# Activations of 128 of 576 tokens from gathered rows of U, and an fp32 gate matrix stored on SP's queue

## The reference, cut to what matters

```
h = rms_norm(x + merged @ w_out)                       # 576 x 2048
s = scores of 8 heads x 2 halves against 128 keys      # top 16 of each, top 16 of the 256 pairs
experts[n, head, k]   (128 experts of 16384 a token), gate = softmax(top_s)
act  = gelu(h[n] . u[experts[n, head, k]])             # u: 16384 x 2048, fp32
out[n] = sum over head, k of gate * act * v[experts]   # v: 16384 x 2048, fp32
```

## Time and profile before

| | us |
|---|---|
| median of 3 runs | 4928.46 (4912.31 to 4931.71) |
| the profiled execution, its own time | 4921.65 |
| its span | 4919.6 |

### The profile page before, as it was taken

The page is one execution under the profiler, slowest core; times in us unless marked ns, Lnnn a source line. Parts: engine busy times, 40 slices in busy tenths (PEclk is TensorE's granted clock), DMA queues, the critical chain, the costliest instruction groups (busy, mean ns, idle before and its releaser), DMA issues.

```text
span 4919.6 us, 84579 instructions
## 1 busy us (share of the span) xinstructions
PE 4749.3 (97%) x35079; PEld 4510.0 (92%) x35079; DVE 2807.5 (57%) x5183; ACT 1217.3 (25%) x1483; POOL 780.0 (16%) x768
## 2 busy tenths in 40 slices
PE   8999999999999899999999999999999999999997
PEld 8999888888999899999999999999988888888887
DVE  3332643223343668878888863333366666776667
ACT  3212533322121212222222221212222222222223
POOL 1010012320000000000011000000054334434430
PEclk9999999999999999999999999999999999999999
DMA  6333246763445334434555554344488778877873
GB/s 191 104 112 99 64 158 216 235 202 102 134 128 144 71 72 105 109 100 118 131 141 141 133 133 109 102 106 107 162 318 304 303 302 302 310 265 302 305 298 110
DMA packets 474042, 842.18 MB, mean 171 GB/s; under 512 B 45201, under 2 KB 307345, under 8 KB 431512
## 3 DMA queue, kind: packets, MB, share of 16 engines
q1 hardware_dynamic: 400272, 502.55, 33.9%
q0 software_dynamic: 67968, 325.20, 19.0%
q10 hardware_dynamic: 5520, 10.49, 0.7%
HBM read 739.48 MB, written 94.14 MB: 169 GB/s over the span
## 4 chain that ended last, share of the span: by engine, by line
PE 80%; DMA 8%; DVE 6%; issue 3%; ACT 2%; SPq 1%; ACTq 0%; DVEq 0%
PE pair L1795 61%; PE pair L2218 10%; DMA v_raw<-in_peer_v_dram 7%; PE pair L1759 2%; DVE v_lo L1672 2%; PE pair L2199 2%; DVE main L1690 2%; ACT v_hi L1086 1%; PE pair L2152 1%; PE pair L1966 1%; ACT w_hi L776 1%; PE pair L1831 1%; PE pair L2009 1%; SPq L537 0%; PE pair L2106 0%
## 5 line engine op out<-in xcount | busy, mean ns | idle before, releaser
L1795 PE MATMUL pair<-act_hi,w_hi 128*128 128x288 f32 x7616 | 1653.9, 299 | 32.2 <-DVE act_lo L1219 12.1
L1795 PE MATMUL pair<-act_hi,w_lo 128*128 128x288 f32 x7616 | 1635.9, 297 | 0.0
L1795 PE MATMUL pair<-act_lo,w_hi 128*128 128x288 f32 x7616 | 1635.5, 296 | 0.0
L1795 PEld LDWEIGHTS pair<-act_hi,w_hi 128*128 128x128 f32 x7616 | 1229.0, 190 | 71.1 <-issue 64.8
L1795 PEld LDWEIGHTS pair<-act_lo,w_hi 128*128 128x128 f32 x7616 | 1232.9, 190 | 0.0
L1795 PEld LDWEIGHTS pair<-act_hi,w_lo 128*128 128x128 f32 x7616 | 1232.1, 189 | 0.0
L2218 PE MATMUL pair<-wx_hi,v_hi 128*128 128x384 f32 x2016 | 691.0, 343 | 52.7 <-DVE main L1690 44.6
L2218 PE MATMUL pair<-wx_hi,v_lo 128*128 128x384 f32 x2016 | 680.6, 338 | 0.0
L2218 PE MATMUL pair<-wx_lo,v_hi 128*128 128x384 f32 x2016 | 679.9, 337 | 0.0
L1690 DVE TENSOR_TENSOR main<-pair,main 128x384 f32<-128x384 f32 x1024 | 546.3, 553 | 221.5 <-PE pair L2218 206.6
L1159 DVE TENSOR_TENSOR w_lo<-w_raw,w_hi 128x2048 fp32r<-128x2048 f32 x103 | 236.2, 2293 | 749.1 <-ACT w_hi L776 747.4
(11 more groups left out here) (294 smaller groups left out, 3402.9 us busy)
## 6 DMA issues: line engine op xcount, KB each, us to landing
w_raw<-in_peer_u_dram SPq DMA_DIRECT2D x512, 256.0 KB
v_raw<-in_peer_v_dram SPq DMA_DIRECT2D x128, 1024.0 KB
w_raw<-in_w_in_dram SPq DMA_DIRECT2D x64, 1024.0 KB
gelu_dram<-tmp SPq DMA_DIRECT2D x128, 288.0 KB, 2.6
gmat_dram<-gmat POOLq DMA_DIRECT2D x24, 1024.0 KB, 11.5
a_back<-gelu_dram SPq DMA_DIRECT2D x128, 192.0 KB
g_back<-gmat_dram SPq DMA_DIRECT2D x128, 192.0 KB
w_raw<-in_w_out_dram SPq DMA_DIRECT2D x16, 1024.0 KB
```

The costliest lines, as they stand in the source:

```text
L1795: op = m_(pair[out][:, hf, 0:TH], w[:, k, :], x[:, k, hf * TH:(hf + 1) * TH], start=(starts and k == ks[0] and i == 0), stop=(ends and k = ...
```

## The change

1. The dense U stage keeps tokens 0 to 447 (`TU`). One matmul has 448 columns and one bank instead of two of 288 in two; a tile has 48 matmuls. Two tiles share `pair[0]`; gelus of 448 columns are stored.
2. The last 128 tokens get their activations from gathered rows: the first two tiles let PE turn h of these tokens to rows (high and low), stored in `h_dram`. From tile 31 on, for each token i, POOL gathers 128 rows of U (1 MB, two buffers), SP loads the token's two rows of h (16 KB, one buffer), PE spreads them over 128 partitions into four banks (`spread_h`: 4 matmuls of 512 columns) and DVE multiplies and reduces (`dot`). There are 4 in 3 tiles, over 96 tiles, at k = 3 and k = 11 of a tile. `spread_h(i)` waits for h and for dot i-1; `load_h(i+1)` for `spread_h(i)`; the gather of i+2 for dot i. One gelu at the end makes all of them, and only 64 tokens gather their cells.
3. The blocks of tokens are selected in the order 3, 4, 0, 1, 2, and the row numbers are computed as soon as their block is there.
4. The gate matrix is made in fp32, without the split: two one-hot operations a token, 8 fp32 matmuls of 128 columns, one ACT copy, no DVE addition, single buffers. One group stands after every second tile from tile 31 to 125. SP stores it, each 32 tokens in four quarters, one after every second tile and the last four at the end, ahead of the loads for the value stage.
5. The loops of the stage are written out.

```diff
+SEL_ORDER = (3, 4, 0, 1, 2)
+DOT_TILE = G_FIRST + 1
+TU = 448
+U_RING, H_RING = 2, 1
+def dots_of(n):
+    n -= DOT_TILE
+    return list(range(4 * n // 3, 4 * (n + 1) // 3)) if 0 <= n < 3 * N_SU // 4 else []
+def group_of(n):
+    return (n - DOT_TILE) // 2 if 0 <= n - DOT_TILE < 2 * N_G and (n - DOT_TILE) % 2 == 0 else None
...
 SP
+            def store_gates(m, piece):
+                t = slice(m % 2 * GB // 2, (m % 2 + 1) * GB // 2)
+                j = slice(piece * PK // 4, (piece + 1) * PK // 4)
+                sp.wait_ge(gm_ev, 4 * (m + 1))
+                sp.dma_start(gmat_dram[:, j, m * GB // 2:(m + 1) * GB // 2], gmat[:, j, t]).then_inc(gm_out[m % 2], 16)
+            for n in range(N_U - 4):
+                if n:
+                    store_gelu(n - 1)
+                if n == DOT_TILE:
+                    sp.wait_ge(h_saved, H_SAVED + 16)
+                    sp.wait_ge(sel_tev, 3 * TB)
+                    for i in range(H_RING):
+                        load_h(i)
+                for i in dots_of(n)[0:1]:
+                    load_h_after(i)
+                sp.wait_ge(u_turn, 2 * (n + 3))
+                load_u(n + 4, n % 2)
+                for i in dots_of(n)[1:2]:
+                    load_h_after(i)
+                m, piece = divmod(n - DOT_TILE - 8, 8)
+                if 0 <= m and piece % 2 == 0:
+                    store_gates(m, piece // 2)
...
+            for piece in range(4):
+                store_gates(11, piece)
...
 POOL
+            for i in range(N_SU - U_RING):
+                pool.wait_ge(dot_done, DOT + i + 1)
+                gather_u(i + U_RING)
...
 DVE
+            def dot(i):
+                dve.wait_ge(h_spread, i + 1)
+                dve.wait_ge(u_row_in[i % U_RING], U_IN + 16 * (i // U_RING + 1))
+                v.tensor_tensor_reduce(out=u_rows[i % U_RING][:, :], in0=quad[:, :, :].rearrange("p a c -> p (a c)"),
+                                       in1=u_rows[i % U_RING][:, :], scale=1.0, scalar=0.0, op0=ALU.mult, op1=ALU.add,
+                                       accum_out=e_act[:, N_CELL + i:N_CELL + i + 1]).then_inc(dot_done, 1)
+            for n in range(G_FIRST, N_U - 1):
+                g = group_of(n)
+                for part in range(2):
+                    u_low(n + 1, (n + 1) % 2, part, n + 1 == N_U - 1)
+                    if g is not None:
+                        one_hots(g, part)
+                    for i in dots_of(n)[part:part + 1]:
+                        dot(i)
...
 PE
+            def expert_tile(n, hooks):
+                if n >= 2:
                     pe.wait_ge(a_gelu, n - 1)
+                for k in range(KD):
+                    if k % 8 == 0:
+                        pe.wait_ge(u_lo, n * 2 + 1 + k // 8)
+                    if k in hooks:
+                        hooks[k]()
+                    for i, (w, x) in enumerate(((w_hi, act_hi), (w_hi, act_lo), (w_lo, act_hi))):
+                        op = m_(pair[0][:, n % 2, 0:TU], w[n % 2][:, k, :], x[:, k, 0:TU],
+                                start=(k == 0 and i == 0), stop=(k == KD - 1 and i == 2))
+            def spread_h(i):
+                pe.wait_ge(h_in[i % H_RING], H_IN + 16 * (i // H_RING + 1))
+                if i:
+                    pe.wait_ge(dot_done, DOT + i)
+                for c in range(4):
+                    op = m_(quad[:, c, :], ones_r[:, :], h_row[i % H_RING][:, c * 512:(c + 1) * 512], start=True, stop=True)
+                op.then_inc(h_spread, 1)
```

More of the change, by code:

```diff
@@ L1070, in _ @@
-            gate_block(0, True)
-            with act.Fori(1, TV // GB) as blk:
-                gate_block(blk)
-            with act.Fori(0, (N_U - G_FIRST - N_G) // 2 - 1) as hh:
-                for s in range(2):
-                    n = hh * 2 + (G_FIRST + N_G + s)
-                    u_high(n + 1, 1 - s)
-                    gelu(n, s)
-            u_high(N_U - 1, 1)
-            gelu(N_U - 2, 0)
+                q, i = divmod(n, SEL_TILES)
+                if q < TB and i == SEL_TILES - 1:
+                    gate_exp(SEL_ORDER[q])
@@ L1081, in value_high @@
+                gelu(n)
+                if 1 <= q <= TB and i == (1 if q < TB else 0):
+                    take_selected(SEL_ORDER[q - 1])
+                if n < 2:
+                    take_h(2 * n)
+                    take_h(2 * n + 1)
+                if group_of(n) is not None:
+                    take_gates(group_of(n))
             def value_high(n):
@@ L1657, in _ @@
-            link(v.scalar_tensor_tensor(e_cell[:, 0:P], cell[:, 0:P], float(T), col, ALU.mult, ALU.add),
-                 v.scalar_tensor_tensor(e_cell[:, P:N_SP], cell[:, P:N_SP], float(T), more, ALU.mult, ALU.add))
-            v.scalar_tensor_tensor(e_row[:, :], iaT[:, TV:T], float(P), ibT[:, TV:T], ALU.mult, ALU.add).then_inc(top_done, 1)
-            with dve.Fori(0, (N_U - G_FIRST - N_G) // 2 - 1) as hh:
-                for s in range(2):
-                    for i in range(2):
-                        u_low(hh * 2 + (G_FIRST + N_G + 1 + s), 1 - s, i)
@@ L1664, in _ @@
-            for i in range(2):
-                u_low(N_U - 1, 1, i, last=True)
+            def dot(i):
[4 more added lines that the diff above has]
+                                       accum_out=e_act[:, N_CELL + i:N_CELL + i + 1]).then_inc(dot_done, 1)
@@ L2123, in _ @@
             key_scores(N_PQ - 1)
-            def expert_tile(n, s, first=False):
-                if not first:
+            def expert_tile(n, hooks):
+                if n >= 2:
                     pe.wait_ge(a_gelu, n - 1)
-                pe.wait_ge(u_lo, n * 2 + 1)
-                tile(w_hi[s], w_lo[s], s, range(8), ends=False)
-                pe.wait_ge(u_lo, n * 2 + 2)
-                tile(w_hi[s], w_lo[s], s, range(8, KD), starts=False).then_inc(a_done, 1)
+                for k in range(KD):
[6 more added lines that the diff above has]
+                                start=(k == 0 and i == 0), stop=(k == KD - 1 and i == 2))
+                op.then_inc(a_done, 1)
```

317 lines of the change are left out of this document (164 added, 153 removed).

## The result

The changed kernel takes 5006.46 us (median of 4 runs, 5005.37 to 5010.1), the kernel before 4923.41 in the same comparison (4 runs, 4912.31 to 4931.71). The ratio is 1.0171, interval 1.0148 to 1.0195: slower, where 4898 was forecast, and above the range of 4820 to 4980. The profiled execution took 5005.37 us, its span is 5003.6.

What follows compares the result with a forecast made beforehand. PE alone was taken to bound the U stage, the value stage being mixed, with DVE the bound in selection after the change. Terms -60 - 6 + 25 + 19 - 2 = -24 on 4921.65 gave 4898 us, range 4820 to 4980.

Steps and rivals of the forecast that it cites:

- What bounds; selection: PE alone sets the U stage before; in selection, tiles 0 to 30, DVE becomes the bound: 326 for 386.6 us, -60.
- the sum of the dots' stretch: Tiles 31 to 126: period of 81 us per six tiles, 1300 for 1274.9 us, +25; ends 1220 and 1412.
- PE's own work: Dots' stretch: tile 9.6 us, spread 0.91, gate group 2.2; 71.5 us per six tiles, 1144 in all.
- The waits: PE's waits per six dots' tiles: one-hots 2.4, dot 1, h behind U 4, gate stores 1.2, gathers 1; sum 9.6 us.
- Gate stores on SP's queue: Dots' stretch: quarters of 4096 runs, 4.7 us each, queued before h, cost 1 to 1.5 us in six tiles.
- Into the value stage: After tile 126: last four quarters, `main`, weights and V make PE wait 25 us, less 6 lost before: +19.
- The value stage: In the stage itself POOL issues 128 fewer cell gathers: -2 us, 0 to -15.
- h is late throughout: Rival, dots' stretch: one h buffer loaded behind U and quarters; 5004 at 87 us a period, 4955 at 84.5; chance 0.21.
- break-even of 82.5 us: Period of six tiles in the dots' stretch at which it takes 1324 us, 1.5 us above the forecast period.
- the rival of the clock: Dots' stretch: 32 waits grow to 4 us, each costing 2 to 3 more at lower clock, +64 to +96; 4975; chance 0.09.
- Gathers too slow: Rival, dots' stretch: gathers of 17 us or more, each 1 us more costs 1 us in two dots; 4940 at 18; chance 0.09.
- waits hidden: Rival, much faster: h lands early in the dots' stretch and quarters cost 2.5 us; -113, 4809; chance 0.19.

Runs made afterwards that it cites:

- the filled waits: Changed kernel with 16 matmuls of 448 columns before the wait for h that follows a two-dot tile: 4960.88 us, ratio 1.0102 to the kernel before.
- the fastest kernel: Changed kernel with two early-loaded h buffers, gate groups in one-dot tiles, their product one tile behind the one-hots: 4754.92 us, ratio 0.9681 to the kernel before.

## Why the prediction was wrong, by its own steps

**What bounds; selection.** Right: -67.4 for -60, within its ends, with DVE as the bound. The 7 us between them come from a slip in the count. From gelu 0 to gelu 30 are 30 tiles, five blocks of 63.3 us, 316.5; the 9.6 added to it is a tile too many. Measured are 62.3 us on average for four blocks and 70.1 for the first, in which h is turned. DVE's work was 315 us, not 306, and it had 5 us of idle time in 320.

**The step that failed is the sum of the dots' stretch**: +25 forecast, +144.4 measured. With its ends of 1220 and 1412 us it leaves out what came. Its three terms, with the fully busy stretch of 1190.9 us as the measure of PE's own work (the forecast's is 1302 here and not 1300, by rounding):

| term | forecast | measured | off by |
|---|---|---|---|
| PE's work at full clock | 1144 | 1190.9 | +47 |
| PE idle | 158 (16 x 9.6 + 4) | 135.9 | -22 |
| longer work at the lower clock | 0 | 1283.1 - 1190.9 = 92.2 | +92 |
| sum | 1302 | 1419.0 | +117 |

- *The clock.* This term was put at nothing, and it is the error that turned the sign: the span grew by 84 us, and without these 92 it would have shrunk by 8. The records agree with the 92 by another way, 185 us of work at the lower level. I had the mechanism as a rival, with 0.09, and wrote that waits of 3.1 us and below stay free of it, reading a threshold into one wait of 4.77 us. That row only shows that a wait of 4.77 us pays; it says nothing of shorter ones. Here waits above 3 us pay, some 2.7 us for one of 3.73; most of those of 0.9 to 1.9 behind two-dot tiles pay too, and the filled waits show the cause. The section "Part 1: The HAM clock gate" of the Trainium skill's "TensorE: Matmul & The Clock Gate", that a gap between bursts can put the array back to half rate, agrees with the clock of 0.50 behind the wait of 3.73 us.
- *The waits.* Those for h came out as forecast: 98 us, for 16 x (4 + 1.2 + 1) = 99 with the gate stores and the gathers that were to lengthen them. The parts differ a little: behind two-dot tiles 3.3 to 4.0 us in 19 cases and 0.9 to 1.9 in 11, for 3.1 and 0.9 in turn, and 15.7 us inside them. Ahead of the first spread PE waited 15 us, not 4. The one-hots took 20.7 and not 40, as a late PE finds them ready, and the dot 2.3 and not 16. That h waits behind U, for which no row stood before, is shown: ahead of U the kernel runs at 0.9893, behind it at 1.0171. So this step of the forecast held; its price did not. By "Queues, rings and completion order" in "DMA: Bandwidth & Descriptors" of the Trainium skill a DMA engine takes a queue's descriptors in ring order; the trace agrees, with 7.0 us for 16 KB issued 2 us behind a load of U.
- *PE's own work.* This is the second term that was mis-sized. Dense tiles take 9.7 us (9.6 forecast, 10 us over 96 tiles). Spreads take 1.35 us and not 0.91: 128 x 0.44 = 56 us too little. I had priced their columns alone. The two inner steps of a spread have that price (0.23 and 0.24); the surplus lies at its two ends, where PE goes over from 128 rows to 2 and back. Gate groups take 1.8 us (two-dot tiles with one 14.2, without 12.4) and not 2.2: 48 x 0.4 = 19 us too much, as I had divided a row that holds the tail of its last matmul. Together that is the 47.

**Gate stores on SP's queue.** The 1.2 us a period were a guess, and what they do is another thing than I had: the store is issued in 0.4 us, but SP's next issue is held for 4.4 to 10.3 us. That makes most of the 15.7 us of waits inside two-dot tiles, of which 3.5 are left with the stores on ACT's queue; it decided little, as the waits for h were no shorter in all.

**Into the value stage.** The mechanism was right and its size was not: PE waited 17.7 us and not 25, so the step is +14.8 for +22. The last quarters are what delays it, as with the last one stored at tile 107 PE waits 5.0 us there. They took less than forecast: SP issued the four at 3596.08 and `main`, which waits for them, at 3609.86, 13.8 us, where 4 x 4.7 and a landing are 21. `main` took 13.1 us, as forecast.

**The value stage.** -9.3 for -8.

**The rivals.** The measured 5006 lies on the 5004 of "h is late throughout", and not for its reason: that rival wanted 87 us a period made of waits. The period is 88.7, with 8.5 us of idle time in it (9.9 forecast), 5.8 of lower clock and 2.9 of dearer work. So its break-even of 82.5 us was passed by the clock and the spreads. What came is the rival of the clock, in size too (64 to 96 us forecast, 92 measured), but not on its condition: the waits did not have to grow to 4 us. Added to the dearer work it gives what was measured; the forecast had no case for both. "Gathers too slow" and "waits hidden" didn't occur; by its own rule the first would have been 64 us at 18 us a gather, 4962 and not 4940. And the range was too narrow for the chances beside it: it was to leave out a tenth at either side, but the rival at 4809 had 0.19, and of the 0.21 of "h is late throughout" only the milder form, 4955, lies inside.

## What to carry to other kernels

A small load that PE waits for must not be issued behind a large one on the same queue: another order, another buffer or another queue each took 2.5 to 3.5% off this kernel. Price a wait of PE twice, for itself and for the lower clock that can follow it, and take a single long wait in the trace as proof that the price exists, not as its threshold; if a wait can't be removed, even useless matmuls in it paid here, by 0.7%. And put a product that needs another engine's late result into the next tile: that (with a second buffer) was worth 1.8% here, where moving the same work to lighter tiles had lost time.

## What was not expected of the hardware

- SP's next issue behind a store of 4096 runs of 128 bytes is held: the 43 stores of gelus that follow one took 4.4 to 10.3 us to issue in the changed kernel (10.32 at 2508.59), and 0.34 at 2495.94, where no gate store stood ahead. In the fastest kernel they are held for 6.8 to 9.5 us, and nothing waits for it.
- Waits under 2 us were followed by the lower clock in some cases and not in others. With the gate groups in one-dot tiles PE waited 1.2 and 1.7 us in turn before 47 groups, 14 us and more apart, and the records show the lower level only at the stretch's first wait (20.5 us). In the changed kernel waits of 1.04 and 1.48 us, 9 us apart, were followed by it, and with h between SP's wait and U one wait of 1.95 us was and another of 1.95 us was not. What makes the difference stays open.
- Four matmuls of 512 columns from two rows cost 1.35 us, 0.44 more than their columns at the pace of the dense ones.
- In the fastest kernel the DMA share is 0.97 over 1192 us (241 GB/s) and PE waited for a load once, for 0.5 us, where 0.79 in the changed kernel went with 98 us of late loads. The share did not tell; the order on the queue did.
